# Delta turns: the third projection of the short convolution in halves ahead of A2 and of M

## The reference

```python
br_sc = (sc_b * causal_dwconv(sc_c * sc_x, sc_conv_w)) @ w_sc_out
...
o = gated_delta_rule(q, k, v, g, beta)
```

## Time and profile before

| | us |
|---|---|
| median of 3 runs | 1915.46 |
| lowest and highest | 1914.85, 1916.63 |
| profiled execution | 1919.28 |
| its span, first to last instruction | 1917.4 |
| TensorE busy | 1782.5 (93%) |
| VectorE busy | 1312.8 (68%) |
| GpSimd busy | 766.1 (40%) |
| ScalarE busy | 744.9 (39%) |

### The profile page before, as it was taken

How to read it: one execution, slowest core, us unless ns; L and a number is a source line. 1 busy time by engine, 2 the same in 40 slices (tenths; PEclk the granted TensorE clock), 3 DMA queues, 4 the chain that set the end, 5 groups by cost and what they waited for, 6 DMA issues and landing times. The chain is left out here.

```text
span 1917.4 us, 30996 instructions
## 1 busy us (share of the span) xinstructions
PE 1782.5 (93%) x11421; PEld 1572.1 (82%) x11421; DVE 1312.8 (68%) x2754; ACT 744.9 (39%) x1217; POOL 766.1 (40%) x451
## 2 busy tenths in 40 slices
PE   3998988889995998999998999979999999999997
PEld 2766877768874888999998999979998888888886
DVE  5874455533314578787777999856787888777776
ACT  4332232232215233333334767643333333333333
POOL 3333122324431346777772333213454443333330
PEclk8998999989997999999998999989999999999999
DMA  9661100012312227888875999978889999888882
GB/s 345 235 226 34 35 29 30 24 62 93 98 55 99 88 88 251 292 285 289 294 261 179 352 307 333 344 244 296 286 317 332 365 369 362 321 323 326 323 320 111
DMA packets 178687, 432.58 MB, mean 226 GB/s; under 512 B 15752, under 2 KB 91656, under 8 KB 178464
## 3 DMA queue, kind: packets, MB, share of 16 engines
q1 hardware_dynamic: 125088, 273.71, 41.7%
q0 software_dynamic: 36864, 134.23, 19.6%
q10 hardware_dynamic: 16640, 23.36, 3.3%
HBM read 383.54 MB, written 47.71 MB: 225 GB/s over the span
## 5 line engine op out<-in xcount | busy, mean ns | idle before, releaser
L199 POOL DMA_INDIRECT own_rows<-in_peer_v_dram,own_row x128 | 213.5, 1668 | 329.6 <-DVE y_own L1931 310.9
L1405 POOL TENSOR_TENSOR piece_lo<-weight_ring,piece_hi 128x1024 fp32r<-128x1024 f32 x84 | 202.1, 2406 | 150.3 <-ACT piece_hi L1335 150.3
L199 POOL DMA_INDIRECT own_rows<-in_u_rows_dram,own_row x128 | 161.2, 1259 | 240.3 <-DVE own_rows L1628 173.3
L1266 PE MATMUL bank<-h_hi,piece_hi 128*128 128x384 f32 (+1 forms) x672 | 237.4, 353 | 11.4 <-DVE h_lo L1511 4.4
L1266 PE MATMUL bank<-h_lo,piece_hi 128*128 128x384 f32 (+1 forms) x672 | 235.1, 350 | 0.0
L1266 PE MATMUL bank<-h_hi,piece_lo 128*128 128x384 f32 (+1 forms) x672 | 234.9, 350 | 0.0
L1841 PE MATMUL bank<-v_hi,coef_lo 128*128 128x512 f32 x512 | 199.6, 390 | 0.0
L1841 PE MATMUL bank<-v_lo,coef_hi 128*128 128x512 f32 x512 | 199.6, 390 | 0.0
L1841 PE MATMUL bank<-v_hi,coef_hi 128*128 128x512 f32 x512 | 199.2, 389 | 0.1
L1335 ACT ACTIVATE piece_hi<-weight_ring 128x1024 fp32r<-128x1024 f32 x84 | 89.3, 1063 | 252.9 <-PE bank L1266 245.0
L1916 DVE TENSOR_TENSOR v_lo<-weight_ring,v_hi 128x1024 fp32r<-128x1024 f32 x128 | 156.6, 1223 | 24.4 <-ACT v_hi L1872 22.4
(11 more groups left out here) (400 smaller groups left out, 4289.7 us busy)
## 6 DMA issues: line engine op xcount, KB each, us to landing
weight_ring<-in_peer_v_dram SPq DMA_DIRECT2D x128, 512.0 KB, 5.3
weight_ring<-in_peer_u_dram SPq DMA_DIRECT2D x68, 512.0 KB, 4.5
ada<-in_w_ada_dram SPq DMA_DIRECT2D x48, 512.0 KB, 5.8
gate_scratch<-gate_block SPq DMA_DIRECT2D x48, 512.0 KB, 7.2
gate_tiles<-gate_scratch SPq DMA_DIRECT2D x32, 768.0 KB, 6.8
gelu_scratch<-gelu_early ACTq DMA_DIRECT2D x104, 192.0 KB, 4.5
gelu<-gelu_scratch SPq DMA_DIRECT2D x104, 192.0 KB, 5.6
u_early<-in_peer_u_dram SPq DMA_DIRECT2D x36, 512.0 KB, 6.9
```

Source lines behind the costliest of these rows:

```text
L199: pool.indirect_dma_start(own_rows[:, n % R], None, tables[n // NS], bass.IndirectOffsetOnAxis(ap=own_row[:, n % NS:n % NS + 1], axis=0)). ...
L1266: last = nc.tensor.matmul(out, ww[:, n % HR, k, :], x[:, k, 0:nt], start=(k == 0 and m == 0), stop=(k == KT - 1 and m == 2))
L1405: nc.gpsimd.tensor_tensor(w_lo[:, n % HR], w[:, n % WR], w_hi[:, n % HR].bitcast(F32), ALU.subtract).then_inc(lo_ready, 1)
```

## The change

In each turn the third projection stood in two halves, one ahead of M and one behind wT. Now they stand ahead of A2 and ahead of M. VectorE's product `sc_u`, which frees the bank for that projection, moves from behind P1 to behind rv, ahead of L. Nothing else moves; no instruction is added or removed, and the orders of GpSimd, ScalarE and SyncE are the same in both programs.

```diff
                     VA, AA, PA = ...
 
+                    sc_product(3 * tt + 2, slice(0, HJ))
                     level("A2", b0, "AT", "A", lambda g: [PA(f"nearT{g}"), VA("rv"), VA(f"LT{g}"), VA(f"aT{g}")])
...
                     level("P", b0, "PT", None, lambda g: [VA(f"P4{g}")])
 
-                    sc_product(3 * tt + 2, slice(0, HJ))
+                    sc_product(3 * tt + 2, slice(HJ, KT))
                     level("M", b1, "CT", "BT", lambda g: [PA(f"farT{g}"), AA(f"P{g}")])
...
                     last.then_inc(*E.step("wT"))
-                    sc_product(3 * tt + 2, slice(HJ, KT))
                     for c in G2:
...
                     nc.vector.tensor_tensor(rv[:], bank[5][:].rearrange("p (h d) -> p h d", h=H), per_head(cols[:, 1]), ALU.mult).then_inc(*V.step("rv"))
+                    dve.wait_ge(tile_done, N0 + 3 * tt + 2)
+                    nc.vector.tensor_tensor(sc_u, sc_c, sc_ps, ALU.mult).then_inc(sc_mul, 1)
                     for g, banks in ((0, (0, 7, 1)), (1, (2, 3, 5))):
...
                         nc.vector.tensor_tensor(W["PT", g][:], W["AT", g][:], mask("chunk_ident"), ALU.add).then_inc(*V.step(f"P1{g}"))
-                    dve.wait_ge(tile_done, N0 + 3 * tt + 2)
-                    nc.vector.tensor_tensor(sc_u, sc_c, sc_ps, ALU.mult).then_inc(sc_mul, 1)
                     dve.wait_ge(*VA("P11"))
```

## The result

| | before | changed |
|---|---|---|
| median, us | 1915.15 (6 runs) | 1942.06 (6 runs) |
| lowest to highest | 1907.53 to 1916.63 | 1940.21 to 1952.43 |
| profiled execution, its span | 1919.28, 1917.4 | 1942.96, 1941.0 |

The ratio is 1.0159, 95% interval 1.0137 to 1.0181: 26.9 us slower by the medians, 23.6 us by the spans of the two profiles. The prediction said 1943 us.

The account below looks back on a forecast made before the run. TensorE's work plus waits bounds the delta stage's turns, PA2's wait being at bottom GpSimd's chain. Terms of +3.92 plus 2.99 give +6.9 us a turn, +27.6 in four, on the median 1915.46: 1943 us, range 1936 to 1949.

Parts of the forecast that it names:

- Part 1: Ahead of A2, the first half product waits for GpSimd's split of the third projection's weights: +7.75 us idle a turn.
- Part 2: From A2 to the second PA2, TensorE's waits for AT and P1 vanish within the new idle: -3.45 us a turn.
- Part 3: Half product ahead of A2 runs mostly at 1.2 GHz after the idle: +2.0 us a turn, bounds 0 to 3.
- The row of one idle ahead of a projection: Profile row: after 4.74 us idle, a projection's first nine matmuls took 3.98 us at clock 0.50, a cost of 2.0.
- The rival in which the clock stays up: During the idle ahead of A2 the clock stays up or falls too late: +19.7 us, 1935 us; chance 0.05.
- The one in which the low clock lasts into the squarings: Low clock outlasts the half product: +1 us a turn, 1947 us; chance 0.10 together with a late multiply.
- Part 4: Behind wT the second half product leaves, uncovering ScalarE's copies: -2.08 us net; wait ahead of dS0 goes: -0.3 a turn.
- Part 5: VectorE's sc_u, 0.67 us, fits ahead of L: 0 to +0.1 us a turn, taken as 0.
- The sum: All terms together: +6.9 us a turn, +27.6 us in the delta stage's four turns, with nothing giving it back.
- the prediction's own list of signs: Profile signs expected in the delta stage, including a 7.5 to 8 us wait; changed lengths of other stretches would refute it.
- The rival with the other sign: Split ready when the half product starts ahead of A2, so waits are covered: -9.5 us, 1906 us; chance 0.03.
- What was said of the blocked P1: VectorE's second P1 (L883) is held past three GpSimd instructions, ending behind the split at 192.05; PA2 waits for it.

Follow-up runs that it names:

- e1: Changed kernel with GpSimd's split for the third projection moved from behind by_head to ahead of the masks: 1900.29 us against 1914.61 for the kernel before.
- e4: Changed kernel with GpSimd's split for the third projection ahead of the two by_head instructions instead of behind them: 1934.82 us, ratio 1.0115 to the kernel before.
- e7: Changed kernel with 28 unread 128x512 matmuls added ahead of TensorE's wait for the split: 1935.63 us, against 1948.84 for the changed kernel on the same chip.
- e8: Changed kernel run again unaltered, on another chip than its first runs: 1948.84 us against 1916.36 for the kernel before.
- e11: Changed kernel unaltered, one more profiled execution: 1945.25 us.
- e3: Kernel before with only VectorE's multiply sc_u moved ahead of L, TensorE's order as it was: 1914.5 us against 1914.61.
- e2: Kernel before with only GpSimd's split for the third projection moved ahead of the masks: 1907.05 us against 1914.61.

## Why the prediction was right, point by point

- **Part 1, the wait.** Predicted +7.75 us of idle a turn, measured 30.98 in four turns (kk to the half product, 42.09 against 11.11). e1 shows the cause by taking the wait away, e4 by shortening it.
- **Part 2, what the idle swallows.** Predicted -13.8 us in four turns; A2 to P measured -13.7, of which +0.5 is low clock in turn 1.
- **Part 3, the clock.** Predicted +8.0, measured 8.6 in the half products (1.3 us in turn 0 and 2.4 in the others) and 0.5 in the squarings of turn 1. The row of one idle ahead of a projection gave 2.0; the other row, 2.4, was the nearer in three turns of four. e7 confirms the cause. The rival in which the clock stays up is out. The one in which the low clock lasts into the squarings came true in small: 0.5 us in all here, 1.0 in e8 and e11, where it priced 4.
- **Part 4, behind wT.** Predicted -8.3 and -1.2, measured -8.4 and -1.3.
- **Part 5, the multiply.** Predicted 0 to +0.1 us a turn; e3 and the 0.80 against 0.79 us from kk to L say the same.
- **The sum.** Predicted +27.6; the stretches that it names add up to 27.9. The term that it did not have is the clock elsewhere: row sums to kk and dS to oT came out 3.1 us shorter in this execution. By the prediction's own list of signs that is one against it ("if the stage's other stretches change length"). But they do that without the change too: row sums to kk was 12.0 to 12.1 or 13.6 us in all but one of the turns profiled (once 10.4, in e3), and dS to oT 10.6 to 10.7 or 12.2 to 12.3 outside the last turn. In the kernel before, row sums to kk has a granted clock of 0.75 in a turn where it takes 13.60 us and of 0.86 in one where it takes 12.00. The medians, 26.9 us apart, lie between 24.8 and 27.9.
- **The closeness is partly luck.** The terms stand, but that 1943 meets a median of 1942.06 to 1 us says little: on the chip of e8 the same kernel had a median of 1948.84, 32.5 us above the kernel before and at the upper end of the range.
- **A reading that was wrong without effect.** The sum says that no DMA of size runs in these turns. The windows of the half product show a DMA share of 0.35 to 0.61 in the changed kernel, and in the kernel before the half product behind wT (207.57 to 210.52) shows 0.59. TensorE's list of waits names no DMA in either.
- **The rival with the other sign** was priced at 1906 us for the case that the split is ready. e1 makes it ready and takes 1900.3. That is beyond the price by more than the slip that can be named: the price kept the second PA2 at 192.11, held by P1, and in e1 P1 ends 4 us sooner, which is worth 0.46 us a turn, 1.8 in all. The remaining 3.9 us lie inside e1's interval.
- **What was said of the blocked P1** stands only in part. In the changed kernel the longest of the eight P1 still takes 4.66 us, to the end of the split. In e4 the split stands ahead of by_head, and the pair of P1 ends behind the split (186.76) and not behind by_head (188.77). In e1 and e2 it is done during by_head. So P1's end follows the 128-partition split, wherever that stands close behind the masks. Why the second P1, which in the kernel before was due at 187.5, with by_head (8 partitions) just beginning, did not run before the split began at 189.43, the runs do not tell; in e2 it was due at the same point, about 0.3 us into by_head, and ran at once, in 0.50 us. The Trainium skill (SBUF — State Buffer, "Who interferes with whom") lets the later of two such instructions wait until the first finishes. e4 agrees (the pair of P1 ends 0.27 us behind the split, 183.97 + 2.52). In the kernel before and the changed one P1 is held past the end of the instruction ahead of it, into the next but one, so there the measurement goes beyond the page.

## What to carry to other kernels

Before a piece of work is moved forward as a filler, look at every semaphore that it waits for, and at where the engine that releases it does so in its own order: the hidden price is that the filler turns a stall of 3 us into one of 8. Cover is only cover when its inputs are ready; here the same move cost 27 us with the split late, and together with the split early it gained 14, of which 7.6 are the early split's own (e2). And an engine that idles 9 to 19 us in each turn (GpSimd ahead of the masks) while it has a job waiting that others will need soon is the first place to look for time.

## What the runs showed of the hardware

- Filling 6.7 us of TensorE's idle with useless matmuls made the program 6 to 13 us shorter, since the granted clock stayed at 1.00 (e7).
- After one and the same idle of 7.7 us the clock stayed at 0.50 for 2.7 us in one turn and for nearly all of the 5.4 us of the half product in the three others, and so in all four turns of e8 and e11. Where the clock is down differs from one execution to the next of the same program, and with it the time by some us.
- In e4 GpSimd's split took 2.52 us instead of 2.33 where VectorE's P1 was due in front of it, and by_head 2.06 instead of 1.89 in e1 and e2: the delay went in both directions, by 0.2 us for GpSimd and by 2.1 to 4.2 us for VectorE, whose second P1 takes 0.50 us in e1 and e2, 2.56 in e4 and 4.67 in the kernel before. Besides, GpSimd's last mask, beside which the first P1 runs in every kernel here, takes 1.2 us where the others take 0.73; no run separates these two.
